# Finishing the second-last output row in two halves, on three engines

## The reference

```python
x = _layer_norm(DEEPNORM_ALPHA * x + mixed @ w_out[layer], ln1_g[layer], ln1_b[layer])
gate, up = jnp.split(x @ w_gate_up[layer], 2, axis=-1)
ffn = (jax.nn.silu(gate) * up) @ w_down[layer]
x = _layer_norm(DEEPNORM_ALPHA * x + ffn, ln2_g[layer], ln2_b[layer])
```

## Time and profile before

| what | us |
|---|---|
| median of 3 runs | 1261.48 |
| lowest, highest run | 1261.38, 1262.99 |
| span of the profiled execution | 1261.5 |
| TensorE busy | 1226.6 (97%) |
| VectorE busy | 956.2 (76%) |
| GpSimd busy | 664.3 (53%) |
| ScalarE busy | 520.5 (41%) |

### The profile page before, as it was taken

How to read it: one execution, slowest core, us unless ns; L and a number is a source line. 1 busy time by engine, 2 the same in 40 slices (tenths; PEclk the granted TensorE clock), 3 DMA queues, 4 the chain that set the end, 5 groups by cost and what they waited for, 6 DMA issues and landing times.

```text
span 1261.5 us, 17034 instructions
## 1 busy us (share of the span) xinstructions
PE 1226.6 (97%) x6037; PEld 1031.8 (82%) x6037; DVE 956.2 (76%) x1547; ACT 520.5 (41%) x911; POOL 664.3 (53%) x546
## 2 busy tenths in 40 slices
PE   8988999999998999999999999999999999999997
PEld 8967788888887899888778888888888888888885
DVE  3687899999987888537867776766776766565897
ACT  4375322221238898513433323333323333653451
POOL 2240666798788642108778666666666630020744
PEclk9999999999999999999999999999999999999999
DMA  5231222201102112414135445445445448966664
GB/s 201 72 90 32 51 51 59 66 19 51 34 17 51 35 27 76 151 59 158 68 116 177 168 137 180 169 141 166 159 133 192 157 152 290 361 189 195 198 188 164
DMA packets 121404, 157.66 MB, mean 125 GB/s; under 512 B 7252, under 2 KB 81256, under 8 KB 119912
## 3 DMA queue, kind: packets, MB, share of 16 engines
q1 hardware_dynamic: 121320, 156.57, 38.4%
HBM read 109.09 MB, written 40.11 MB: 118 GB/s over the span
## 4 chain that ended last, share of the span: by engine, by line
PE 85%; DVE 8%; ACT 2%; issue 2%; DMA 1%; POOL 0%; DVEq 0%; SPq 0%; ACTq 0%; POOLq 0%
PE banks L694 25%; PE banks L696 25%; PE banks L695 25%; PE banks L908 2%; DVE step_lo L2263 2%; PE banks L959 2%; DVE scores L1905 1%; PE banks L859 1%; PE banks L927 1%; PE banks L928 1%; DVE small L2348 1%; PE banks L710 1%; DVE pt L2002 1%; PE banks L877 0%; PE banks L876 0%
## 5 line engine op out<-in xcount | busy, mean ns | idle before, releaser
L1921 DVE TENSOR_SCALAR_CACHE_REDUCE mask<-scores,small 128x384 bf16<-128x384 f32 (+1 forms) x186 | 163.7, 943 | 1.1
L2263 DVE TENSOR_TENSOR step_lo<-step_raw,step_hi 128x1024 fp32r<-128x1024 f32 x77 | 110.4, 1456 | 57.3 <-ACT step_hi L1455 56.6
L1689 POOL TENSOR_TENSOR ring_lo<-sum,ring_hi 128x512 fp32r<-128x512 f32 x88 | 121.6, 1383 | 56.4 <-ACT ring_hi L1390 56.3
L694 PE MATMUL banks<-act_hi,ring_hi 128*128 128x512 f32 x352 | 137.2, 390 | 0.0
L696 PE MATMUL banks<-act_hi,ring_lo 128*128 128x512 f32 x352 | 137.1, 389 | 0.0
L695 PE MATMUL banks<-act_lo,ring_hi 128*128 128x512 f32 x352 | 137.1, 389 | 0.0
L1689 POOL TENSOR_TENSOR ring_lo<-gu_raw,ring_hi 128x512 fp32r<-128x512 f32 x66 | 94.4, 1430 | 74.8 <-ACT ring_hi L1390 74.8
L1455 ACT ACTIVATE step_hi<-step_raw 128x1024 fp32r<-128x1024 f32 x77 | 81.6, 1061 | 110.8 <-DMA step_raw<-in_w_down 55.7
L1390 ACT ACTIVATE ring_hi<-sum 128x512 fp32r<-128x512 f32 x88 | 55.1, 630 | 161.6 <-POOL sum L1700 61.6
L694 PE MATMUL banks<-step_hi 128*128 128x512 f32 x308 | 120.1, 390 | 0.1
L696 PE MATMUL banks<-step_hi,step_lo 128*128 128x512 f32 x308 | 119.9, 389 | 0.0
(11 more groups left out here) (270 smaller groups left out, 3165.1 us busy)
## 6 DMA issues: line engine op xcount, KB each, us to landing
gu_raw<-in_w_gate_up SPq DMA_DIRECT2D x44, 512.0 KB, 5.2
step_raw<-h_store SPq DMA_DIRECT2D x77, 256.0 KB, 2.9
wd_raw<-in_w_down SPq DMA_DIRECT2D x11, 1024.0 KB, 4.9
h_store<-hid SPq DMA_DIRECT2D x11, 1024.0 KB, 3.9
step_raw<-wd_store SPq DMA_DIRECT2D x44, 256.0 KB, 3.5
wd_store<-wd_raw SPq DMA_DIRECT2D x11, 768.0 KB, 3.4
h_store<-h_sum SPq DMA_DIRECT2D x11, 768.0 KB, 5.4
step_raw<-in_w_down SPq DMA_DIRECT2D x33, 256.0 KB, 3.3
```

The costliest lines, as they stand in the source:

```text
L694: pe.matmul(dst, a[0], b[0], start=first, stop=False)
L1689: pool.tensor_tensor(ring_lo[:, slot], src, ring_hi[:, slot].bitcast(F32), ALU.subtract).then_inc(ring_low, 1)
L1921: c = dve.tensor_scalar(mask[:, part(b)], scores[:, part(b)], threshold(j), 0.0, ALU.is_ge, ALU.add, accum_out=count[:, j:j + 1])
L2263: dve.tensor_tensor(step_lo[n][:], step_raw[n][:], step_hi[n][:].bitcast(F32), ALU.subtract).then_inc(step_low, 1)
```

## The change

Row 6 is cut at column 512. VectorE finishes the left half directly behind the gain of row 6, which is before it takes up the last product (row 7); the right half is scaled by ScalarE and gets its bias from GpSimd, behind GpSimd's root of row 7. VectorE then no longer finishes row 6 between the variance and the gain of row 7. SyncE issues four transfers of half a row instead of one of a whole row and two of halves, in the order: row 6 left, row 7 left, row 6 right, row 7 right.

```diff
-            sp.wait_ge(finished, 1)
-            sp.dma_start(out_rows[ROWS3[6]], y2[:, ROWS3[6], :]).then_inc(stored, 16)
-            for half in range(2):
-                cols_ = slice(half * 512, (half + 1) * 512)
-                sp.wait_ge(finished, 2 + half)
-                sp.dma_start(out_rows[ROWS3[7]][:, cols_], y2[:, ROWS3[7], cols_]).then_inc(stored, 16)
-            sp.wait_ge(stored, 16 * (NB + 1))
+            left, right = slice(0, DM // 2), slice(DM // 2, DM)
+            for q, cols_, ready, value in ((6, left, finished, 1), (7, left, finished, 2),
+                                           (6, right, normed, 2 * NB - 1), (7, right, finished, 3)):
+                sp.wait_ge(ready, value)
+                sp.dma_start(out_rows[ROWS3[q]][:, cols_], y2[:, ROWS3[q], cols_]).then_inc(stored, 16)
+            sp.wait_ge(stored, 16 * (NB + 2))
...
-            def scale_row2(q):
+            def scale_row2(q, first=0):
                 act.wait_ge(gained, NB + q + 1)
                 act.wait_ge(root_ready, NB + q + 1)
-                act.activation(y2[:, ROWS3[q], :], scaled[:, q % 2, :], ACT.Copy, scale=rstd2[:, q:q + 1]
+                act.activation(y2[:, ROWS3[q], first:], scaled[:, q % 2, first:], ACT.Copy, scale=rstd2[:, q:q + 1]
                                ).then_inc(root_scaled, 1)
...
             for q in (4, 5):
                 scale_row2(q)
+            scale_row2(6, DM // 2)
...
-            def add_bias2(q):
+            def add_bias2(q, first=0):
...
-                pool.tensor_tensor(y2[:, b, :], y2[:, b, :], bias2[:], ALU.add).then_inc(normed, 1)
+                pool.tensor_tensor(y2[:, b, first:], y2[:, b, first:], bias2[:, first:], ALU.add).then_inc(normed, 1)
...
                 root2(q)
                 if 1 <= q < 7:
                     add_bias2(q - 1)
+            add_bias2(6, DM // 2)
...
                 if q < NB - 1:
                     apply_gain(q, 0, DM)
                 else:
-                    finish_row(NB - 2, 0, DM)
                     apply_gain(q, 0, DM // 2)
                     apply_gain(q, DM // 2, DM // 2)
+                if q == NB - 2:
+                    finish_row(q, 0, DM // 2)
             finish_row(NB - 1, 0, DM // 2)
             finish_row(NB - 1, DM // 2, DM // 2)
```

## The result

The changed kernel is slower. Its median over seven executions is 1265.76 us against 1261.48, 4.3 us more. The ratio on record is 1.0028, 95% interval [1.0018, 1.0038], or +3.5 us (2.3 to 4.8); it is worked out over the runs and is not the quotient of the two medians, which is 1.0034. The forecast was 1264.2 in a range of 1262.3 to 1264.8, so the time lies 1.0 us above the range. The direction, the mechanism and the sum for the end of the program were right. What failed is the step from that sum to a time with a range: executions of one kernel lie further apart than the range allowed for, and why the changed kernel's lie mostly at the upper end is still open.

The account below looks back on a forecast made before the run. TensorE was 85% of the chain; only the 8.2 us behind its last matmul could move. VectorE's end: +2.16 - 1.20 + 1.03, or +2.00; transfers +0.4 to +0.7; from 1261.5 to 1264.2 us, 8-in-10 range 1262.3 to 1264.8.

Parts of the forecast that it names:

- First meeting: Ahead of the last add, VectorE's left finish of row 6 waits for GpSimd's bias of row 5: +2.16 us.
- the first rival: VectorE, not GpSimd's bias of row 5, goes first; row 6's left half ends 1253.52, end 1262.5 us; chance 0.08.
- The removed finish: Row 6's whole-row finish between variance and gain of row 7 leaves VectorE's path: -1.20 us.
- the second meeting: Near the end, GpSimd's bias of row 6 right goes ahead of VectorE's row 7 left finish: +1.03 us.
- The root: GpSimd's root of row 7 ends 0.41 us behind the left gain of row 7, at 1258.46, not on the path.
- The transfers: At the end, three late half-row transfers instead of two, bound by data: +0.4 to +0.7 us on top of +2.0.
- Chances: Odds for the whole time against a 0.2% (2.5 us) bound: slower 0.50, same 0.47, faster 0.03.

## Why the prediction was right and wrong

- **First meeting**, forecast: who starts first goes first, whole; the left half ends at 1255.61, the add is 2.16 late. Right: it took 2.76 us (forecast 2.8), and the add is 1255.35 - 1253.15 = 2.20 behind the last matmul against 0.04 before, so 2.16 late. The margin that I took as 0.06 is 0.13, since VectorE takes up the root 0.10 behind its end; that makes the first rival, VectorE first, less likely than I had it.
- **The removed finish**, -1.20, and **the second meeting**, +1.03: right. VectorE's last instruction ends 7.69 behind the last matmul (1260.84 - 1253.15) against 5.75 before (1259.08 - 1253.33), +1.94 where 2.00 was forecast; the second meeting alone came out at 1.01. The root ends 0.41 behind the first gain, as worked out, and was on no path.
- **The transfers**, +0.4 to +0.7: right, at 0.71, by the third late half. The issues came closer together than forecast, 0.38 and 0.48 apart, so the last half is issued 0.21 behind VectorE's end (forecast 0.32) and still waits for data.
- **The sum**, forecast +2.7 for the stretch (2.00 and 0.7): measured +2.65, and the changed kernel's four profiles agree within 0.01.
- **The step that failed** is the one that turned the sum into a time and its range. It has two terms. The first was put at nothing: "The sum is made against the span, 1261.5, which is the median of the runs (1261.48) to a few hundredths, so nothing has to be added for what lies around it." That agreement was chance. A time is its span plus 1.8, so the profiled execution took about 1263.3 and belongs to the upper group, while the median that it seemed to match lies in the middle one. Its counterpart of the changed kernel, with the last matmul at 1253.15, took 1265.79, which is 1263.3 + 2.65 - 0.18 for the earlier matmul. By luck this error alone moves the forecast by nothing: put on the median of before, the measured +2.65 gives 1264.1. The second term was mis-sized, and it is the one that put the time outside the range: "above by the run-to-run spread" allowed 0.5 to 0.6 us above the forecast. The groups stand 1.7 us apart, one kernel's executions lie over 4 us apart, and of the three runs that were known one (1262.99) already lay 1.5 above their median. The changed kernel's median fell into its upper group, at 1265.8 instead of 1264.1. Why it did stays open.
- **Chances**: 0.50 for slower by over 0.2%. All four ratios of the changed kernel are at 1.0020 or above. By the stretch alone it would be 1.0021, at the bound itself; the rest goes with the mix of groups, whose cause is open.

The Trainium skill's rule on the shared pair (SBUF — State Buffer, Who interferes with whom) is borne out by these runs in two of its parts: the pair needs two SBUF inputs on VectorE (0.75 us from PSUM beside a running bias, 2.76 from SBUF), and the order of start decides. That the GpSimd instruction has to read SBUF is a part that no run here tests. The Trainium skill's price for a transfer (DMA: Bandwidth & Descriptors, Anatomy of one DMA — SWDGE (gpsimd) path) is given there for transfers of GpSimd's queue, while these are issued by SyncE. By an estimate from it, the end would be 0.4 us later than it is (1260.20 + 3.8 + 0.4 against 1264.00).

## What to carry to other kernels

Before an instruction of VectorE is moved into an idle gap, look at what GpSimd does in that gap: if both read two SBUF tensors, the gap is not free, and the later one waits for the whole of the earlier; one operand of VectorE's in PSUM took the pair apart here. Work handed to GpSimd at the end of this kernel was paid by the next two-tensor instruction of VectorE. Put a sum on a time of the same execution as its rows, and look first how far the executions of one kernel lie apart: here the forecast of a change of 0.2% was right to 0.05 us in one stretch of the profile, while the times of one kernel lie 4 us apart.

## What the runs showed of the hardware that I had not expected

ScalarE's scaling of a half takes 0.72 us, not 0.63, and VectorE's take-up of GpSimd's root is 0.10 us for the finish, which waits on two semaphores, against 0.03 for the instruction at 525.28; whether the second semaphore is the reason isn't shown. GpSimd's root ends 0.41 us behind the VectorE instruction beside which it started, and holds up the next one by nothing: beside a half gain it takes 0.99, beside a whole instruction 1.52. And the granted clock near 635 us differs between executions of one program, behind the same idle waits of TensorE.
